# A third buffer for the products of keys, and their sums one half group later, in a one-step hybrid decoder on one core

## What is computed

```python
z = rmsnorm(x, ln1_w) @ w_in  # q, k, v of 8 attention heads x 64; q, k, v, gates of 4 mLSTM heads x 128
attn = moba_attention(qa, k_all, v_all, q_start)      # own block of 256 keys + the top 3 past blocks
h, C, n, m = mlstm_chunkwise(qm, km, vm, i_pre, f_pre, C0, n0, m0)
x = x + concat(attn, norm(h) * sigmoid(om)) @ w_out
x = x + square(relu(rmsnorm(x, ln2_w) @ w_up)) @ w_down
y = rmsnorm(x, lnf_w)
```

## Time and profile before

| | |
|---|---|
| median of 3 runs | 740.16 us (737.09 to 741.37) |
| profiled execution | 740.26 us |
| its span in the trace | 738.5 us |
| TensorE busy | 701.6 us, 95% |
| VectorE busy | 452.8 us, 61% |
| ScalarE busy | 296.7 us, 40% |
| GpSimd busy | 316.2 us, 43% |
| granted TensorE clock, mean | 0.975 |
| HBM read | 92.92 MB, 135 GB/s over the span |

### The profile page before, as it was taken

One profiled execution on the slowest core, in us unless ns is written; L12 is line 12 of the kernel. 1 busy time (PEld: TensorE's weight loads), 2 busy tenths in 40 slices (PEclk: granted clock), 3 DMA queues, 4 the chain that ended last, 5 costly groups with the idle time before them and its releaser, 6 DMA issues.

```text
span 738.5 us, 15194 instructions
## 1 busy us (share of the span) xinstructions
PE 701.6 (95%) x5561; PEld 652.2 (88%) x5561; DVE 452.8 (61%) x894; ACT 296.7 (40%) x568; POOL 316.2 (43%) x229
## 2 busy tenths in 40 slices
PE   5999799797999999889989999999999999999996
PEld 5989688686878787579989999999999999999996
DVE  4387878766452438353779776574857557485133
ACT  5342554533445122114655634335343433534322
POOL 5226977831232335143723742508053250805531
PEclk9999999998999999989999999999999999999999
DMA  8726898742556869903311133313323231333203
GB/s 244 217 57 211 264 288 246 207 146 77 169 136 213 264 202 193 263 26 120 116 58 57 58 116 114 115 58 116 114 90 96 98 114 58 115 115 104 68 1 117
DMA packets 88633, 100.41 MB, mean 136 GB/s; under 512 B 5374, under 2 KB 64338, under 8 KB 88570
## 3 DMA queue, kind: packets, MB, share of 16 engines
q1 hardware_dynamic: 74566, 92.91, 41.1%
q10 hardware_dynamic: 14004, 6.67, 3.7%
HBM read 92.92 MB, written 6.64 MB: 135 GB/s over the span
## 4 chain that ended last, share of the span: by engine, by line
PE 80%; DVE 8%; ACT 3%; DMA 3%; issue 2%; POOL 2%; SPq 1%; ACTq 0%; DVEq 0%; POOLq 0%
PE acc L895 7%; PE acc L896 6%; PE acc L897 6%; PE acc L1376 5%; PE acc L1375 5%; PE acc L1377 5%; PE acc L1341 4%; PE acc L1342 4%; PE acc L1343 4%; PE scr L1376 3%; PE scr L1377 3%; PE scr L1375 3%; PE scr L1341 3%; PE scr L1342 3%; PE scr L1343 3%; PE acc L1181 2%
## 5 line engine op out<-in xcount | busy, mean ns | idle before, releaser
L895 PE MATMUL acc<-act_hi,w_hi 128*128 128x256 f32 (+1 forms) x416 | 124.6, 299 | 0.6 <-DVE zT L2455 0.5
L896 PE MATMUL acc<-act_lo,w_hi 128*128 128x256 f32 (+1 forms) x416 | 119.9, 288 | 0.0
L897 PE MATMUL acc<-act_hi,w_lo 128*128 128x256 f32 (+1 forms) x416 | 119.5, 287 | 0.0
L1972 POOL TENSOR_TENSOR h_lo<-relu,h_hi 128x520 fp32r<-128x520 f32 x32 | 44.5, 1391 | 167.5 <-ACT h_hi L1763 167.1
L1927 POOL TENSOR_TENSOR prod<-kv,Qb 128x1024 f32<-128x1024 f32 x32 | 82.9, 2616 | 42.5 <-DVE S L2158 24.5
L1461 POOL TENSOR_TENSOR w_lo<-raw,w_hi 128x1024 fp32r<-128x1024 f32 x20 | 47.6, 2381 | 95.8 <-ACT w_hi L1454 95.8
L895 PEld LDWEIGHTS acc<-act_hi,w_hi 128*128 128x128 f32 x416 | 81.1, 195 | 7.4 <-issue 5.2
L896 PEld LDWEIGHTS acc<-act_lo,w_hi 128*128 128x128 f32 x416 | 81.1, 195 | 0.0
L897 PEld LDWEIGHTS acc<-act_hi,w_lo 128*128 128x128 f32 x416 | 80.8, 194 | 0.0
L2474 DVE TENSOR_TENSOR xT<-acc,xT 128x260 f32<-128x260 f32 x64 | 26.4, 427 | 55.1 <-PE acc L1377 55.1
L2455 DVE TENSOR_TENSOR zT<-acc,rstd 128x264 f32<-128x264 f32 (+1 forms) x56 | 23.5, 423 | 55.7 <-PE acc L897 49.7
(11 more groups left out here) (420 smaller groups left out, 2336.9 us busy)
## 6 DMA issues: line engine op xcount, KB each, us to landing
kv<-in_cache_k_dram SPq DMA_DIRECT2D x64, 256.0 KB, 3.1
kv<-in_cache_v_dram SPq DMA_DIRECT2D x64, 256.0 KB, 3.2
raw<-in_w_up_dram SPq DMA_DIRECT2D x16, 1024.0 KB, 5.4
raw_d<-in_w_down_dram SPq DMA_DIRECT2D x12, 1024.0 KB, 5.1
raw<-in_w_in_dram SPq DMA_DIRECT2D x14, 512.0 KB, 5.9
raw<-in_w_in_dram SPq DMA_DIRECT2D x7, 1024.0 KB, 6.9
x_tok<-in_x_prompt_dram SPq DMA_DIRECT2D x8, 512.0 KB, 8.5
raw<-in_w_out_dram SPq DMA_DIRECT2D x4, 1024.0 KB, 6.3
```

What stands on the lines that cost most here:

```text
L895: pe.matmul(out, w_hi[:, slot, k, :], hi[k][:, cols], start=(n == 0), stop=False)
L896: pe.matmul(out, w_hi[:, slot, k, :], lo[k][:, cols], start=False, stop=False)
L897: mm = pe.matmul(out, w_lo[:, slot, k, :], hi[k][:, cols], start=False, stop=(n == KT - 1))
L1972: pool.tensor_tensor(h_lo[:, t, :], relu2[:, t % 2, :], h_hi[:, t, :].bitcast(F32), ALU.subtract).then_inc(s_hs_lo, 1)
```

## The change

`prod3`, two pages wide, is laid over `pv_masked` and `pv_tok`, and takes every third product; `prod[:, 0]` and `prod[:, 1]` take the others. Product n waits for sum n - 3 instead of n - 2. The sum of product n stands two slots behind it, at most in slot 30: sums 0 and 1 in slot 10, 2 in 11, 3 and 4 in 12, 5 in 13, 6 and 7 in 14, 8 in 15, and so on; 28 and 29 in slot 29, 30 and 31 in slot 30. No slot of a product moves.

```diff
--- before.py
+++ after.py
@@ -184,7 +184,7 @@
     at(pv_slot(7) + 3, ("pv_end",))
     for n in range(4 * NS):
         at(chunk_slot(n), ("score", *divmod(n, 4)))
-        at(chunk_slot(n) + 1, ("kred", *divmod(n, 4)))
+        at(min(chunk_slot(n) + 2, 30), ("kred", *divmod(n, 4)))
         if n % 4 == 1 and n >= 5:
             at(chunk_slot(n), ("qb", n // 4 + 1)) if n // 4 + 1 < NS else None
     for h in range(MH):
@@ -501,8 +501,9 @@
         pTs = pT_a, pT_b
         vm_tok, _ = place("vm_tok", [P, NT, MD + 1])
         km_tok, _ = place("km_tok", [P, NT, MD])
-        pv_masked, _ = place("pv_masked", [P, AW])
+        pv_masked, pv_masked_at = place("pv_masked", [P, AW])
         pv_tok, _ = place("pv_tok", [NS, AW])
+        prod3, _ = place("prod3", [P, 2 * AW], at=pv_masked_at)
         S, _ = place("S", [P, NS, PAGES, AH])
         Qb, qb_at = place("Qb", [P, 2, AW])
         vs_split, _ = place("vs_split", [LOW + NS, AW], F32R, at=qb_at)
@@ -687,6 +688,10 @@
             n = JOBS[key]
             eng.wait_ge(scr_free[n % 4], n // 4 + 1)
 
+        def product(n):
+
+            return prod3[:, :] if n % 3 == 2 else prod[:, n % 3, :]
+
         def page_used(eng, b, j):
 
             eng.wait_ge(s_pv_used, PAGES * b + j + 1)
@@ -1922,9 +1927,9 @@
                         evacuated(pool, "qb", b, 0)
                     for j in (2 * c, 2 * c + 1):
                         pool.wait_ge(kv_in[j], 16 * (b + 1))
-                    if n >= 2:
-                        pool.wait_ge(s_kred_ok, n - 1)
-                    pool.tensor_tensor(prod[:, n % 2, :].rearrange("p (j n) -> p j n", j=2),
+                    if n >= 3:
+                        pool.wait_ge(s_kred_ok, n - 2)
+                    pool.tensor_tensor(product(n).rearrange("p (j n) -> p j n", j=2),
                                        kv[:, 2 * c:2 * c + 2, :],
                                        Qb[:, b % 2:b % 2 + 1, :].to_broadcast([P, 2, AW]), ALU.mult)\
                         .then_inc(s_kmul_ok, 1)
@@ -2156,7 +2161,7 @@
                     n = 4 * b + c
                     dve.wait_ge(s_kmul_ok, n + 1)
                     dve.tensor_reduce(S[:, b, 2 * c:2 * c + 2, :].rearrange("p j h -> p (j h)"),
-                                      prod[:, n % 2, :].rearrange("p (g d) -> p g d", d=AD), AX.X, ALU.add)\
+                                      product(n).rearrange("p (g d) -> p g d", d=AD), AX.X, ALU.add)\
                        .then_inc(s_kred_ok, 1)
                 elif name == "sm_prep":
                     out = full(dve, "sm_prep", 0)
```

## The result

The changed kernel takes 743.16 us (median of 15 runs, 738.82 to 747.54) beside 741.14 us of the kernel before (15 runs, 737.09 to 742.80): **1.0039 times as long, 95% interval 1.0021 to 1.0057**, some 2.9 us. (The ratio is estimated from all the runs; the two medians alone are 2.0 us apart, 1.0027.) A second set of runs on another chip gave 1.0038 (1.0023 to 1.0053); there the medians are 3.0 us apart. Forecast were +1.3 us, and with a chance of 0.57 a time that can't be told from no change (about 0.5%).

The account below looks back on a forecast made before the run. TensorE is busy 95%, so only its waits, such as for scratch banks VectorE empties late, can be won back; GpSimd decides. +0.7 + 1.2 - 0.6 = +1.3 us on 740.26 gave 741.5, range 735.5 to 746.5.

Parts of the forecast that it names:

- (a): Front, to VectorE's slot 9: product 2 starts near 47.5 us and holds scan L2120 until 50.4, +2.4 us.
- The bound at which a scan is left alone (+1.1): Front: scan L2120 untouched beside product 2; the split of 49.30 waits until 50.4 instead, +1.1 us.
- (b): Slots 9 to 13: VectorE takes back the 2.4 us; first emptying of scores at 74.35 instead of 75.44, -1.1 us.
- (d): Clock: one low stretch moves behind 99 us, onto the path, after a longer ks_tok wait; 0 to 1.6, taken +1.2 us.
- (c): Slots 13 to 19: extra sum in slot 14, splits of 14 and 16 may meet products; +0.7 us, range -1.0 to +2.5.
- (e): Slots 19 to 27: TensorE waits for nothing, GpSimd has slack; sums, splits and loads shift along, 0 us.
- (f): Slots 26 to 29: pT_a comes 1.1 us earlier, two sums precede the split of slot 28; taken -0.6 us.
- (g): End of the sums, buffer overlay: free of cost; last two sums in slot 30, no DMA, instruction or semaphore added.
- One sign of being right: Whole products' line: GpSimd's idleness for sums would be well below 24.5 us.
- splits behind products: Slower rival, slots 12, 14, 16, 28: splits wait for products, up to 5.2 us on VectorE; about +6, 746; chance 0.24.
- Its deciding point: Slots 14 and 16: the slower rival decides once their splits take over 3 us each.
- sums off the path: Faster rival, front to slot 28: scan not held or load hidden, split of slot 28 free; -5.6 us, 734.7; chance 0.19.

Follow-up runs that it names:

- Product 2 held: The changed kernel, but product 2 also waits until VectorE's rows of gates are done: 1.0038 times the kernel before.
- the second trace: Profile of the changed kernel, unaltered, from its second set of runs on another chip; span 744.6 us, set's ratio 1.0038.
- the last sums back: The changed kernel with sums 28 to 31 one slot behind their products as before: 1.0009 times the kernel before.
- product 11 behind its split: The changed kernel with product 11 waiting for the split of slot 16 (w_lo of tile 11): 1.0033 times the kernel before.
- the first trace: Profile of the changed kernel from its first set of runs, the shortest of its 15 executions: 738.82 us.

## Why the prediction held, and where it did not

**(a) Right to the tenth of a microsecond.** The scan is held behind product 2 (3.30 us) and the copy of slot 6 comes at 52.79. Product 2 held gives 1.21 us again. The bound at which a scan is left alone (+1.1) falls.

**(b) Right.** The split of slot 12 was made in 1.23 us at 69.25, in GpSimd's gap; product 4 started at 70.30; the first emptying of scores came at 74.23 (forecast 74.35, before 75.44), and TensorE's wait of 1.53 us is gone. The next one, of 2.26 us, is cut to 1.3 ((d) took about 1).

**(c) Right as a range.** Split of slot 14 at 78.95 (forecast 79.0), done at 80.9 (81.1). Split of slot 16 asked for at 89.0 (89.3). The forecast put product 11 ahead of it and, for the doubt, went half way back; it is a matter of 0.03 and 0.26 us in the two traces. Slot 19 came out 0.4 earlier and 1.9 later, around the +0.7, within -1.0 to +2.5. What the step left out: tokv 0 waits for the copy of slot 17, behind sums 9 and 10.

**(d) Right in the place of the low stretch, not in what leads to it.** The low stretch after 84 us is gone, and the one behind 97 us is there in the second trace (twice 3.4 us, slot 20 at +3.1), not in the first (-0.4). Forecast +1.9 at that place. The traces with product 2 held, the last sums back, both, and product 11 behind its split have it too, once or twice; the first trace is the only one of six without it. The wait for v_tok ahead of it was to be about 3 us and is 1.7 and 1.2; in the second trace the 2.12 us ahead of tokv 0, which the step doesn't have, come first.

**(e) Right**: slots 20 to 28 keep their distances to 0.1 us.

**(f) Wrong in sign in both traces, by the clock.** The wait for pT_a went as forecast. That for pT_b rose from 2.4 to 3.5, but only because TensorE comes to it earlier: slot 28 takes 10.6 us where it took 11.4, a gain of 0.8 beside the 0.6 forecast. Then a second low stretch came behind it, and slot 29 takes 4.9 and 5.2 us instead of 3.9. Slots 28 to 30 so take 15.6 and 15.8 us instead of 15.3, +0.3 to +0.5 where -0.6 was taken. The traces with product 2 held and with product 11 behind its split have the same sums there and one low stretch, and take 14.6 and 14.3. So the sign goes with the low stretches of an execution.

**(g) The step that failed.** It put the end of the row of sums at nothing: "the last two sums stand together in slot 30, ahead only of the gate matmul a slot later". That looked at sums 30 and 31 and not at 28 and 29, which move into slot 29. That they stand behind a copy for which VectorE idles, and product 31 and a split behind them, is +1.5 us in both traces and 2.2 us by the run with the last sums back. It is about as large as the difference between +1.3 and +2.9. Who stands behind a moved sum was followed for slots 9 to 16 and not to the end of the row.

**The sum.** In the first trace the parts to slot 31 come out at -0.4 (c, d), +0.3 (f) and +1.5 (g), +1.4 in all beside the forecast +1.3. That they add up so near is luck, since no part has its forecast size; in the second trace they are +3.1, +0.5 and +1.5, +5.1 in all. One sign of being right was missed as well: GpSimd's idleness for sums was to be well below 24.5 us and is 25.7, since the later sums take back what the third buffer gives (20.3 us with the buffer alone).

**The rival "splits behind products"** had the sign right and the mechanism small. (Its "about +6" is less than its terms add up to, 5.2, 1.6 and 2.4, and the forecast does not say why.) The eleven splits between 62 and 156 us take 24.8 us where they took 22.8:

```profile
L1466 DVE TENSOR_TENSOR w_lo<-raw,w_hi 128x1024 fp32r<-128x1024 f32 x11 | 24.8, 2258 | 12.9 <-ACT w_hi L1459 12.9
```

2.0 us more. That most of it lies in VectorE's slack is read from its idleness for w_hi, 12.9 us beside 7.0, and not shown by a run. Its deciding point, slots 14 and 16 both over 3 us, was met at 16 only (1.9 and 3.2 in the second trace), and putting products 26 and 28 behind their splits (with sum 29 a slot later) won nothing in the median.

**The rival "sums off the path"** needed the front free and got nothing from it (product 2 held, 1.0038). Its gain exists, though, and depends on where the sums go: 0.9965.

Open: where the front's 2.4 us go. The four kernels with product 2 held are 0.00 to 0.12% below the same kernels without, in no pair beyond the intervals. In the traces the lead of 2.1 us at slot 9 is 1.2 to 2.5 us at slot 19 in three of these pairs, and gone at slot 31 in two of them (116.7 beside 116.3, 116.8 beside 116.4). That ScalarE's chain to v_tok takes its place fits the waits (0.7 before, 1.2 to 1.7 in all others), but no run took that chain away. Open too is the rest of the 2.9 us beyond the wait for att_o.

## What to carry to other kernels

A fixed amount of work in an in-order queue costs by what stands behind it: measured against thirty-two sums of 1.2 us one slot behind their products, the same sums two slots behind cost +0.9%, and with a third buffer -0.35% when some were set into the idle time ahead of instructions that wait for another engine. Read for each moved instruction which copy or emptying follows it before its engine idles next, and do it to the last one; the ends of a regular pattern are where it meets other work. A deeper buffer alone bought nothing here (1.0013): it cut VectorE's waits for products from 7.3 to 4.8 us, and it started product 2 beside a scan that the product held up.

## What the runs showed that was not expected

- A tensor_tensor_scan with both inputs in SBUF was held by a GpSimd tensor_tensor for the product's whole remaining time: 3.30 instead of 1.21 us in the changed kernel's traces, 1.21 with product 2 held. No row of before had shown it; the forecast took it from a neighbouring row. The Trainium skill (SBUF — State Buffer, "Who interferes with whom") says that a VectorE instruction with two SBUF inputs contends with a GpSimd instruction that reads SBUF. The trace agrees: the scan beside product 2 takes those 3.30 us.
- Two instructions ready within 0.3 us of each other on VectorE and GpSimd went in one order in the trace with slot 19 at 55.6 and in the other in the trace with 57.9. Ahead of them, product 4 waited 2.72 and 2.90 us for its pages, and the low clock stretches stood elsewhere. The kernel's times spread over 8.7 us after the change and 5.7 before (15 runs each), but in the second set over 4.7 and 4.7, so that the change makes the times spread is not shown.
- Low clock stretches (0.50, 1.2 GHz) come and go between executions of one kernel: between 94 and 105 us the changed kernel has none in the first trace and 6.8 us of them in the second, and near 394 us one of 3.4 us in the second alone.
